# Hybrid decoder step: a sample block's softmax work spread over eight slots, and a prompt unit's small product behind the next unit's scores

## What is computed

```python
def fox_prompt(q, k, v, logf):            # causal, 8 heads of 64, blocks of 128 queries
    def block(args):
        i, qi, di = args
        sc = jnp.einsum('bqhd,bkhd->bhqk', qi, k) * scale
        sc = sc + di[:, :, :, None] - dk[:, :, None, :]
        sc = jnp.where(kpos[None, :] <= qpos[:, None], sc, -jnp.inf)
        p = jax.nn.softmax(sc, axis=-1)
        return jnp.einsum('bhqk,bkhd->bqhd', p, v)

def fox_sample(q, k, v, logf, k_past, v_past, logf_past):   # 4096 past tokens per sample, in 32 pages
    sp = jnp.einsum('bqhd,bkhd->bhqk', q, k_past) * scale + d_new[...] + rev[...]
    sn = ...                               # the same over the 4 new keys, causal
    p = jax.nn.softmax(jnp.concatenate([sp, sn], axis=-1), axis=-1)
    out = einsum(p[..., :n_past], v_past) + einsum(p[..., n_past:], v)
```

## Time and profile before

| | |
|---|---|
| median of the runs (lowest, highest) | 2012.65 us (2010.44, 2016.42) |
| the profiled execution's own time | 2018.6 us |
| its span | 2016.9 us |
| mean granted TensorE clock | 0.977 of full speed |
| busy: PE, DVE, ACT, POOL | 93%, 43%, 22%, 12% |
| the slot loop | about 70 to 547 us of the span |
| the slots with prompt units | about 272 to 540 us |

### The profile page before, as it was taken

How to read it: one execution, slowest core, us unless ns; L and a number is a source line. 1 busy time by engine, 2 the same in 40 slices (tenths; PEclk the granted TensorE clock), 3 DMA queues, 4 the chain that set the end, 5 groups by cost and what they waited for, 6 DMA issues and landing times.

```text
span 2016.9 us, 33708 instructions
## 1 busy us (share of the span) xinstructions
PE 1876.5 (93%) x12473; PEld 1121.2 (56%) x12473; DVE 861.9 (43%) x1921; ACT 440.3 (22%) x1017; POOL 249.4 (12%) x381
## 2 busy tenths in 40 slices
PE   6999998888999999999999998987999999999994
PEld 4677655555488868888874487444333333333331
DVE  5644467777656523333344647245111111111115
ACT  3111124444301011101110305131222222212213
POOL 0203333333100000000000000000111111111110
PEclk9999999999999999999999999996999999999997
DMA  7859999999911140210121205344999999999966
GB/s 255 277 169 343 354 337 364 352 339 347 331 63 65 44 154 11 63 53 11 55 74 63 87 1 183 121 171 177 372 381 382 374 373 376 371 372 374 371 222 264
DMA packets 208164, 458.57 MB, mean 227 GB/s; under 512 B 18721, under 2 KB 47418, under 8 KB 207618
## 3 DMA queue, kind: packets, MB, share of 16 engines
q1 hardware_dynamic: 177554, 365.30, 50.8%
q0 software_dynamic: 30448, 91.13, 12.8%
HBM read 432.44 MB, written 32.17 MB: 230 GB/s over the span
## 4 chain that ended last, share of the span: by engine, by line
PE 82%; DVE 6%; ACT 4%; DMA 4%; issue 3%; DVEq 1%; SPq 0%; ACTq 0%; POOLq 0%; POOL 0%
PE ps L1338 20%; PE ps L1691 11%; PE ps L1722 6%; PE ps L1167 6%; PE ps L1403 6%; PE ps L1702 6%; PE ps L1432 5%; PE ps L1731 3%; PE ps L1182 3%; PE ps L1544 2%; PE ps L1290 2%; PE ps L1270 2%; PE ps L1148 1%; DVE kt L2230 1%; DMA vpage<-in_cache_v 1%
## 5 line engine op out<-in xcount | busy, mean ns | idle before, releaser
L1691 PE MATMUL ps<-gu,xgT 128*64 128x512 f32 x1024 | 228.7, 599 | 0.6 <-ACT xgT L2046 0.6
L1338 PE MATMUL ps<-xnT,ring 128*128 128x264 f32 x768 | 184.5, 392 | 3.2 <-ACT xnT L741 1.9
L2230 DVE STREAM_TRANSPOSE kt<-kraw 128x1024 f32<-128x1024 f32 x128 | 151.1, 1219 | 34.5 <-DMA kraw<-in_cache_k 25.3
L1338 PEld LDWEIGHTS ps<-xnT,ring 128*128 128x128 f32 x768 | 147.8, 193 | 30.5 <-ACT xnT L741 2.2
L876 POOL DMA_DIRECT2D vpage<-in_cache_v x228 | 122.4, 537 | 291.6 <-PE ps L1290 233.6
L3053 DVE TENSOR_TENSOR sig_a<-ps,sig_a 128x256 f32<-128x256 f32 x32 | 13.6, 425 | 322.9 <-ACT sig_a L2050 322.9
L1691 PEld LDWEIGHTS ps<-gu,xgT 128*64 128x64 f32 x1024 | 71.1, 138 | 133.0 <-issue 130.2
L1722 PE MATMUL ps<-wd,hidT_a 128*64 128x512 f32 x512 | 116.9, 598 | 20.2 <-ACT hidT_a L2056 11.2
L1702 PE MATMUL ps<-gu,xgT 128*32 128x512 f32 x1024 | 115.8, 592 | 0.0
L1167 PE MATMUL ps<-xnT,early 128*128 128x352 f32 x320 | 101.2, 472 | 4.4 <-DVE xnT L2174 4.4
L1167 PEld LDWEIGHTS ps<-xnT,early 128*128 128x128 f32 x320 | 60.6, 194 | 38.2 <-issue 8.7
(11 more groups left out here) (482 smaller groups left out, 2945.9 us busy)
## 6 DMA issues: line engine op xcount, KB each, us to landing
kraw<-in_cache_k SPq DMA_DIRECT2D x256, 256.0 KB, 5.3
wd<-in_w_expert_down SPq DMA_DIRECT2D x31, 2048.0 KB, 21.5
gu<-in_w_expert_gate SPq DMA_DIRECT2D x30, 2048.0 KB, 20.3
gu<-in_w_expert_up SPq DMA_DIRECT2D x30, 2048.0 KB, 25.1
vpage<-in_cache_v POOLq DMA_DIRECT2D x228, 256.0 KB, 5.8
ring<-in_w_in SPq DMA_DIRECT2D x12, 1024.0 KB, 8.1
yy<-y_d SPq DMA_DIRECT2D x16, 512.0 KB, 10.4
early<-in_w_in SPq DMA_DIRECT2D x6, 1024.0 KB, 11.7
```

The source lines that it names most:

```text
L1338: last = nc.tensor.matmul(bank(R.bank(name, f, q))[:, 0:QT], weight[:, k], src[:, k, cols], start=k == 0, stop=k == HK - 1)
L1691: last = nc.tensor.matmul(bank(0)[h * BA:(h + 1) * BA, :].rearrange("p (x n) -> p x n", x=2), src[:, k, 0:BA], weight[:, k, :, h * DE // 2 ...
L2230: nc.vector.transpose(kt[n % 2].rearrange("p c e s -> p (c e s)")[:, x * 1024:(x + 1) * 1024], kraw[n % 2].rearrange("p c d -> p (c d)")[: ...
```

## The change

`turn_sample_probs` and `exp_pages` are cut in two halves of four units. The exponentials of the first half stay in the slots with n % 8 == 0, those of the second half and of the new keys go to n % 8 == 1; the first half is turned in slot n % 8 == 1, the second and the new keys' in n % 8 == 3. Each half waits only for its own exponentials and for the values of the four units that it overwrites. `st_ready` now counts two per block. The maxima are joined (`join_tops`) behind the slot's prompt work and not ahead of it, `spread_queries` moves to n % 8 == 4 at the end of the slot, and `turn_keys` stands ahead of the turn of the probabilities. In the prompt, the product at L1249 becomes `spread_sums` and stands behind the next unit's scores and turned probabilities; on DVE `take_prompt` changes places with `biased`.

```diff
@@ -525,12 +525,12 @@
             if n == END:
                 R.add("dve", "po", NU - 1, banks=(4,))
             for k, p in halves(n):
-                if p == 0 and k:
-                    R.add("dve", "po", k - 1, banks=(4,))
                 if k + 1 < NU and p < len(chunks(k + 1)):
                     add_scores(k + 1, p)
                 for g, j0, nj in turn_groups(k, p):
                     R.add("act", "pt", k, p, g, banks=TURNS)
+                if p == 0 and k:
+                    R.add("dve", "po", k - 1, banks=(4,))
             for item in items(n):
                 R.add("act", *item, banks=(0, 1, 4))
             if n == 5:
@@ -866,7 +866,7 @@
             elif place == 4:
                 R.read(eng, "sp", NSU - 1)
             elif place == 5:
-                eng.wait_ge(st_ready, DB)
+                eng.wait_ge(st_ready, 2 * DB)
 
         def load_values(eng, n):
 
@@ -1244,6 +1244,9 @@
                     for p in range(2):
                         nc.tensor.matmul(bank(4)[p * HD:(p + 1) * HD, 0:P], vtok[:, j, hp * P + p * HD:hp * P + (p + 1) * HD],
                                          probT[p][:, j, :], start=j == 0, stop=j == i)
+
+            def spread_sums(k):
+
                 pe.wait_ge(f_diag, k + 1)
                 for p in range(2):
                     last = nc.tensor.matmul(bank(4)[p * HD:(p + 1) * HD, P:2 * P], onesw, diag[p], start=True, stop=True)
@@ -1283,7 +1286,7 @@
 
                 b, u = n // SU, n % SU
                 pe.wait_ge(v_in[value_place(n)], 64 * values_in(n) + 64)
-                pe.wait_ge(st_ready, b + 1)
+                pe.wait_ge(st_ready, 2 * b + 1 + u // (SU // 2))
                 if u == 0:
                     R.pe_free(pe, "so", b)
                 for j in range(4):
@@ -1311,13 +1314,15 @@
                 if n == PROMPT0 - 1:
                     prompt_scores(0, 0)
                 if n == END:
-                    weigh_prompt(NU - 1)
+                    weigh_prompt(NU - 1), spread_sums(NU - 1)
                 for k, p in halves(n):
                     if p == 0 and k:
                         weigh_prompt(k - 1)
                     if k + 1 < NU and p < len(chunks(k + 1)):
                         prompt_scores(k + 1, p)
                     turn_probs(k, p)
+                    if p == 0 and k:
+                        spread_sums(k - 1)
                 for item in items(n):
                     do_item(*item)
                 if n == 5:
@@ -1885,13 +1890,14 @@
                     copy(("pt", k, p, g), probT[p][:, j0:j0 + nj, :],
                          lambda b: b[:, 0:nj * P].rearrange("p (j x) -> p j x", j=nj))
 
-            def exp_pages(b):
+            def exp_pages(b, r):
                 act.wait_ge(s_max, b + 1)
+                x = sprob[b % 2][:, r * 512:(r + 1) * 512]
+                nc.scalar.activation(x, x, ACT.Exp, bias=negmax[:, b:b + 1], accum_out=sums[:, b, r:r + 1]
+                                     ).then_inc(s_exp, 1)
+
+            def exp_new(b):
                 act.wait_ge(side_ready, SNEW_READY)
-                for r in range(2):
-                    x = sprob[b % 2][:, r * 512:(r + 1) * 512]
-                    nc.scalar.activation(x, x, ACT.Exp, bias=negmax[:, b:b + 1], accum_out=sums[:, b, r:r + 1]
-                                         ).then_inc(s_exp, 1)
                 nc.scalar.activation(pnew[b % 2], snew[:, b, :], ACT.Exp, bias=negmax[0:QH, b:b + 1],
                                      accum_out=sums[0:QH, b, 2:3]).then_inc(s_exp, 1)
 
@@ -1921,7 +1927,9 @@
                 if KOUT0 <= n < KOUT0 + TILES:
                     copy_key_rows(n - KOUT0)
                 if SU <= n < NSU + SU and n % SU == 0:
-                    exp_pages(n // SU - 1)
+                    exp_pages(n // SU - 1, 0)
+                if SU <= n < NSU + SU and n % SU == 1:
+                    exp_pages(n // SU - 1, 1), exp_new(n // SU - 1)
             def keep_first(name, f, q, after, kept=kept_c):
 
                 if after is not None:
@@ -2345,23 +2353,27 @@
                 nc.vector.tensor_tensor_reduce(out=sprob[b % 2][:, u * PAGE:(u + 1) * PAGE], in0=bank(3)[:, 0:PAGE],
                                                in1=rev[b % 2][:, u * PAGE:(u + 1) * PAGE], scale=1.0, scalar=-3e38,
                                                op0=ALU.add, op1=ALU.max, accum_out=tops[:, b, u:u + 1]).then_inc(R.by["dve"], 1)
-                if u == SU - 1:
-                    dve.drain()
-                    for g in range(4):
-                        nc.vector.tensor_reduce(crest[:, g:g + 1], tops[g * QH:(g + 1) * QH, b, :], AX, ALU.max)
-                    dve.drain()
-                    for g in range(4):
-                        last = nc.vector.tensor_reduce(negmax[g * QH:(g + 1) * QH, b:b + 1], crest, AX, ALU.max, negate=True)
-                    last.then_inc(s_max, 1)
-
-            def turn_sample_probs(b):
-
-                dve.wait_ge(s_exp, 3 * b + 3)
+
+            def join_tops(b):
+
+                dve.drain()
+                for g in range(4):
+                    nc.vector.tensor_reduce(crest[:, g:g + 1], tops[g * QH:(g + 1) * QH, b, :], AX, ALU.max)
+                dve.drain()
+                for g in range(4):
+                    last = nc.vector.tensor_reduce(negmax[g * QH:(g + 1) * QH, b:b + 1], crest, AX, ALU.max, negate=True)
+                last.then_inc(s_max, 1)
+
+            def turn_sample_probs(b, r):
+
+                dve.wait_ge(s_exp, 3 * b + (1, 3)[r])
                 if b:
-                    dve.wait_ge(v_used, b * SU)
-                flat = sprobT.rearrange("p u x -> p (u x)")
-                nc.vector.transpose(flat, sprob[b % 2])
-                nc.vector.transpose(pnewT[b % 2], pnew[b % 2]).then_inc(st_ready, 1)
+                    dve.wait_ge(v_used, b * SU - (SU // 2, 0)[r])
+                half = slice(r * 512, (r + 1) * 512)
+                last = nc.vector.transpose(sprobT.rearrange("p u x -> p (u x)")[:, half], sprob[b % 2][:, half])
+                if r == 1:
+                    last = nc.vector.transpose(pnewT[b % 2], pnew[b % 2])
+                last.then_inc(st_ready, 1)
 
             def mask_own(b):
 
@@ -2375,8 +2387,6 @@
             for n in range(NSU + LAG):
                 if 0 < n <= NSU:
                     join_scores(n - 1)
-                if n % SU == 0 and n + SU < NSU:
-                    spread_queries(n // SU + 1)
                 if n == PROMPT0 - 1:
                     biased(0, 0)
                 if n == END:
@@ -2384,17 +2394,23 @@
                 if n < 3:
                     take_forget(n)
                 for k, p in halves(n):
+                    if k + 1 < NU and p < len(chunks(k + 1)):
+                        biased(k + 1, p)
                     if p == 0 and k:
                         take_prompt(k - 1)
-                    if k + 1 < NU and p < len(chunks(k + 1)):
-                        biased(k + 1, p)
                     if p == 1:
                         invert_sums(k)
                 if n == 5:
                     take_new()
+                if 0 < n <= NSU and n % SU == 0:
+                    join_tops(n // SU - 1)
+                turn_keys(n + 2)
                 if SU < n < NSU + SU and n % SU == 1:
-                    turn_sample_probs(n // SU - 1)
-                turn_keys(n + 2)
+                    turn_sample_probs(n // SU - 1, 0)
+                if SU < n < NSU + SU and n % SU == 3:
+                    turn_sample_probs(n // SU - 1, 1)
+                if n % SU == 4 and n + SU < NSU:
+                    spread_queries(n // SU + 1)
                 if 2 * SU < n < NSU + LAG - 1 and n % SU == 1:
                     mask_own(n // SU - 2)
             near, far = slice(0, HT), slice(HT, NT)
```

## The result

The changed kernel takes **2021.55 us** (median of 10 runs, 2018.46 to 2029.14), the kernel before 2013.15 us (10 runs beside them). The ratio is 1.0041, with an interval of 1.0029 to 1.0052, so it is slower by 8.3 us (5.8 to 10.5). The forecast was 2007.3 us with a range of 1998 to 2018; the rival that ends on the slow side, "the late load decides", had said 2021 us. The profiled execution of the changed kernel took 2020.54 us.

What follows compares the result with a forecast made beforehand. Bound by three nearly balanced resources (PE, DVE, DMA) plus PE's waits between them. Middle -9.6 us (7.6 + 4 - 2), loop's end +5.4, fifth block -1.2: -5.4 us from 2012.65, about 2007.3 us, range 1998 to 2018 us.

Steps and rivals of the forecast that it cites:

- What bounds the kernel: Slot loop, 272 to 508 us: nothing is full; PE, DVE and DMA nearly balance, plus the waits between them.
- Maxima and queries away from the slot's head: Slots of completed blocks: 3.4 us off the path ahead of PE's 2.04 us wait; all 7.6 us of waits go.
- Half turns and the product: Slots after a completed block: DVE some 3.7 us earlier, product moved; 4 of 7.2 us of diagonal waits gained.
- What is late next: Middle, 272 to 508 us: PE's waits for values and keys grow in a shorter stage, costing 2 us.
- The loop's end: After slot 67's last turn: SP loads unit 59 10.4 us later, the next stage starts 5.4 us later.
- The fifth block: Slots 64 and 65: same relief as the other blocks, half of a block's share, 1.2 us gained.
- The sum: Whole kernel: -9.6 + 5.4 - 1.2 = -5.4 us, taken from the median of 2012.65 us.
- C: Loop's end: SP's queue is held by the last turn, next stage 10.4 us later; +8.4 us, 2021 us; chance 0.13.
- B: DMA engines are the floor at 361 GB/s: middle gains 7.8 us, end costs 6.9; 2011.7 us; chance 0.25 including last rival.
- D: Middle gives nearly everything: all 14.8 us of waits go and none grow; -13.7 us, 1999 us; chance 0.17.
- The change does not do what it says: Taking-out still holds DVE, nothing moves in the slots after; -2 us; counted within the DMA-floor rival's 0.25.

Runs made afterwards that it cites:

- softmax alone: Changed kernel with the product and `take_prompt` in their old places, late load included, against the kernel before: 2023.98 us, ratio 1.0039.
- product alone: Kernel before with only `spread_sums` moved behind the next scores and turns and `take_prompt` behind `biased`: 2020.9 us, ratio 1.0034.
- late load alone: Kernel before, with only the load of unit 59 waiting for DVE's signal at the end of slot 67: 2023.88 us against 2014.19, ratio 1.0042.
- SP's order: Kernel before, with SP issuing unit 61 and the weights ahead of unit 59: 2013.29 us, ratio 1.0002.
- the repaired version: Changed kernel, last block's second half turned in slot 66, unit 61 and weights issued ahead of unit 59: 2012.13 us, again 2011.68 us; ratio 0.9986 both times.
- softmax alone with the old end: Kernel before with only the samples' softmax spread, last block in its old slots, product unmoved: 2014.44 us, ratio 0.9997.
- the last run: Second measurement of the changed kernel with last turn in slot 66 and unit 61 and weights ahead of unit 59: 2011.68 us against 2013.98, ratio 0.9986.

## Why the prediction was wrong

Two steps failed: the term for what is late next, which left 2 us for waits that took back most of the middle's gain, and the size of the loop's end. Against the forecast of -5.4 us the runs are 13.7 us higher. The middle gave about 4 us and not 9.6 (5.6 us of the miss), the end cost 8.8 us and not 5.4 (3.4 us), the fifth block gave nothing (1.2 us), and 3.5 us are left over. With the end at its real cost and the middle as forecast, the kernel would still have been 2 us faster: it takes both for the sign.

**What bounds the kernel** was read rightly: a stage of three resources that nearly balance, with PE's waits between them, and an end that hangs on SP's queue.

**Maxima and queries away from the slot's head** (7.6 us taken). The mechanism was right. The waits for turned probabilities fell by 5.0 us, to 2.6 us in four pieces of at most 0.8 us; at the completed block of slot 40 ACT waits 1.46 us for the prompt's maximum, where the earlier trace rows had 3.42. The softmax alone has 2.2 us of these waits and the product alone 8.8, so it is this edit that does it. In size 5.0 of the 7.6 us went in this profile.

**Half turns and the product** (4 of 7.2 us taken). The waits for `diag` went wholly, 7.2 us. But my reason, that DVE is 3.7 us earlier and so the long ones go, is refuted by the softmax alone: there DVE is earlier and they grew to 13.8 us. It is the product's move that takes them away, and it does so only together with the softmax edit; alone it took the same waits away and ended in 431.4 us, with more time at half clock, and cost 6.8 us in the runs. The terms don't add; I had summed them.

**What is late next** (2 us taken) is the step of the middle that failed, and the larger one. I named values and keys but looked at PE's own waits for values, which hardly grew (6.7 to 7.2 us with the `kraw` row). The keys are waited for by DVE, in whose queue the maxima stand behind the keys' turn, and come to PE under the name `ftop`: 2.0 to 6.3 us in this profile, 8.6 and 8.9 us in two others. Of the 14.8 us of waits, 12.2 went, 4.8 came back as these two, and the middle won 7.0 us in this profile and about 4 in the mean, not 9.6. That keys in flight are what holds DVE is read from the traces; no run gave the keys more room (a third key buffer, or fewer loads beside them), so what sets their arrival is not shown beyond the 404 GB/s above.

**The loop's end** (+5.4 us taken, +8.8 measured) was right in mechanism and too small. Its first half was right to 0.1 us: the last turn was forecast 28.9 us behind unit 63's scores (529.6 less 500.7) and ended 29.0 us behind them (521.70 less 492.7). The size of the rest was off. From there to the projection I had 23 us: 8.5 MB at 384 GB/s and 1 us. It took 26.3 us: 2.1 us until the loads ran at full rate (for the 1 us that I had put in no run stands), and 24.24 us at 371 GB/s, which is 9.0 MB. That is 3.3 us, the whole error of this term. The rate of a 4.7 us stretch was no rate for 24 us. I had also not followed unit 63's values, for which PE waited 5.12 us of it; for the input itself, which I had expected to be waited for by 5 us or more, it waited 1.52 us.

**The fifth block** (1.2 us taken) brought no relief of its own: the end of 55.3 us is that of the late load alone, 55.2.

**The sum.** By this profile it is -7.0 + 8.8 = +1.8 us, and the spans say 1.9. The runs say +8.3. The first profiles of both kernels were unlike draws of the middle: with its mean, -4, the sum is +4.8 us. The 3.5 us that are left I can't place: outside of the two parts the four profiles of both kernels take 1536.8 to 1540.7 us. A good part is how profiled executions fall. The first one of the kernel before took 5.5 us more than the median of its runs (2018.6 against 2013.15), that of the changed kernel 1.0 us less; with the 1.7 us by which the old order's executions are slow on average, the sum is +6.5 us, inside the measured 5.8 to 10.5. The late load alone costs 8.5 us in the runs and 8.7 in the profiles (55.2 against 46.5, the mean of the kernel before, twice, and of it with SP's order), so the middle is what seems worth little in the changed kernel's runs; the repaired version is 2.8 us faster. What is left stays open.

**The rivals.** C was right in mechanism and place: the last turn came 10.7 us later behind unit 63's scores than before, and the projection kept its distance from it but for 1.8 us (26.3 against 28.2 us). In size it was right by luck (+8.4 forecast, +8.3 measured): it had 10.4 us for the end and 2 us from the middle, where the profiles have 8.8 and 4. Its condition was that the middle gives less than 4.4 us, and the mean of 4 only just meets it. What spoke for it, that SP already waited 6.4 us there, should have weighed more than the free DMA room: the room is before the wait ends, and can't be used by what is queued behind it. B fell: 403 us of a later stage of the changed kernel run at 375 GB/s, and the kernel before has the same 375 GB/s there, so I could have seen it.

```profile
1412.00:1815.00 403.00, 392.79 (x2448) 134.12 (x2448) 68.35 (x135) 86.37 (x180) 65.87 (x68) 1.00 1.03 375
```

So 361 GB/s is no floor, in the slot loop neither, with 404 GB/s from 308 to 316 us. What B had right is that the DMA engines are full while DVE waits for keys (300 to 316 us). The Trainium skill's page "DMA: Bandwidth & Descriptors", section "Where 436 GB/s comes from", has the HBM side bind at about 358 GB/s for transfers between HBM and SBUF; the trace disagrees, with 375 GB/s over 403 us on one core that works alone. D fell with the waits for keys. "The change does not do what it says" fell too: every instruction moved as stated.

## What to carry to other kernels

When work that frees a buffer moves later, look at the queue of the load that waits for it: its whole tail moves with it, and DMA room that lies before the wait's end is lost. Let the loads that don't need the buffer pass, and release the last block sooner than the steady ones; where the load isn't late, the order won nothing. Where two resources are nearly full, freed waits come back under another name; look for them on the engine that turns or copies the arriving data, not only on the one that is timed. And before a gain of 4 us is read from a profile, see how far that execution lies from the median of the runs.

## What was not expected of the hardware

PE's clock can add to what shorter waits win, or take it. I set PE's pauses of 0.9 us and more from 272 to 545 us in the fourteen profiles beside the granted clock just behind them. Of 77 pauses of 0.9 to 1.0 us, one was followed by a stretch at 1.2 GHz; of 54 from 1.0 to 1.75 us, five; of 43 from 1.75 to 2.5 us, 24; of the 23 longer ones, all. Of 143 pauses of 0.5 to 0.9 us 22 were followed by one too, but for 15 of these a longer pause stood close by. The row of slot 35 above shows it: after 4.15 us of waiting, the scores took 2.42 us, where the same four matmuls had taken 1.13 us at 306.23 us in the same profile. So the same sum of waits costs more in long pieces than in short ones. The stretches behind the pauses of over 2.5 us were 6.2 us long on average; a pause of 1.75 to 2.5 us brought 2.6 us at half clock on average, counting those that brought none, and one of 1.0 to 1.75 us 0.3 us. The softmax alone with the old end has no more idle time of PE than before (31.7 against 32.2 us between 272 and 508 us), but 34 us at half clock there, where the kernel before has 17; its middle is the longest, 432.8 us. The product alone, above, is a second such case. It is also how the pause of 2.74 us in slot 64 came to cost so much. The same pause does not always give the same answer: 2.04 us was followed by the lower level in slot 64 of the last run, and not in slot 41 of the kernel before.
